# Turning X on VectorE and masking the keys on GpSimd in the levels of a delta-rule scan

## The reference

```python
a_mat = jnp.eye(CHUNK) + jnp.einsum('bhnid,bhnjd->bhnij', kb, kc) * decay * strict   # kb = k * beta
sol = lax.linalg.triangular_solve(a_mat, rhs, left_side=True, lower=True)
attn = jnp.einsum('bhnid,bhnjd->bhnij', qc, kc) * decay

def step(S, xs):                       # per chunk
    v_new = u_c - w_c @ S
    o_c = qd_c @ S + att_c @ v_new
    S = S * gt_c + kt_c.T @ v_new
```

## Time and profile before

| | us |
|---|---|
| median of 3 runs | 1614.75 |
| lowest, highest | 1612.74, 1620.44 |
| the profiled execution | 1610.06 |
| its span | 1608.2 |

### The profile page before, as it was taken

How to read it: one execution, slowest core, us unless ns; L and a number is a source line. 1 busy time by engine, 2 the same in 40 slices (tenths; PEclk the granted TensorE clock), 3 DMA queues, 4 the chain that set the end, 5 groups by cost and what they waited for, 6 DMA issues and landing times.

```text
span 1608.2 us, 33676 instructions
## 1 busy us (share of the span) xinstructions
PE 1552.5 (97%) x13961; PEld 1473.6 (92%) x13961; DVE 1064.3 (66%) x1529; ACT 798.2 (50%) x1200; POOL 372.0 (23%) x387
## 2 busy tenths in 40 slices
PE   6999999899899999999999999999999999999998
PEld 6898989699899999988899999999996799899998
DVE  6785456473888835755888748665557866676653
ACT  7764343554555545454555545444444256653432
POOL 0014443005156620003266421221100000211210
PEclk9999899999999999999999999999999999999999
DMA  7463120354455353642455455555743543455553
GB/s 269 160 190 102 44 69 3 112 182 169 185 181 182 135 180 128 244 143 79 161 181 173 162 200 209 191 176 171 241 157 105 210 150 139 157 175 192 183 168 120
DMA packets 44367, 256.50 MB, mean 159 GB/s; under 512 B 5680, under 2 KB 7840, under 8 KB 21984
## 3 DMA queue, kind: packets, MB, share of 16 engines
q1 hardware_dynamic: 39696, 233.26, 41.9%
q0 software_dynamic: 4416, 20.60, 4.4%
q10 hardware_dynamic: 144, 1.05, 0.2%
HBM read 252.68 MB, written 2.22 MB: 158 GB/s over the span
## 4 chain that ended last, share of the span: by engine, by line
PE 78%; DVE 8%; issue 7%; ACT 4%; DMA 2%; POOL 1%; ACTq 0%; DVEq 0%; SPq 0%; POOLq 0%
PE bank L437 21%; PE bank L438 21%; PE bank L439 21%; PE bank L1264 3%; DVE w_lo L310 2%; ACT w_hi L307 2%; DMA sq<-rows_scratch_q 1%; PE bank L641 1%; DVE rs L594 1%; DVE mix L600 1%; PE bank L1434 1%; DVE w_spare L1337 0%; PE bank L1426 0%; PE bank L1441 0%; PE bank L455 0%
## 5 line engine op out<-in xcount | busy, mean ns | idle before, releaser
L437 PE MATMUL bank<-work_r,w_hi 128*128 128x256 f32 (+2 forms) x3232 | 918.2, 284 | 10.2 <-DVE w_lo L310 6.0
L438 PE MATMUL bank<-work_r,w_hi 128*128 128x256 f32 (+2 forms) x3232 | 909.9, 282 | 0.0
L439 PE MATMUL bank<-work_r,w_lo 128*128 128x256 f32 (+2 forms) x3232 | 909.7, 281 | 0.0
L310 DVE TENSOR_TENSOR w_lo<-ring,w_hi 128x2048 fp32r<-128x2048 f32 (+1 forms) x231 | 497.3, 2154 | 313.4 <-ACT w_hi L307 313.3
L437 PEld LDWEIGHTS bank<-work_r,w_hi 128*128 128x128 f32 x3232 | 610.0, 189 | 23.4 <-issue 12.0
L307 ACT ACTIVATE w_hi<-ring 128x2048 fp32r<-128x2048 f32 (+1 forms) x231 | 408.0, 1767 | 445.3 <-PE bank L439 445.2
L438 PEld LDWEIGHTS bank<-work_r,w_hi 128*128 128x128 f32 x3232 | 609.8, 189 | 0.3
L439 PEld LDWEIGHTS bank<-work_r,w_lo 128*128 128x128 f32 x3232 | 609.6, 189 | 0.0
L1652 POOL TENSOR_TENSOR work<-work 128x272 f32<-128x272 f32 (+1 forms) x44 | 92.6, 2104 | 131.1 <-ACT work L1614 131.1
L1640 DVE SCALAR_TENSOR_TENSOR work<-work,params_sb 128x272 f32<-128x272 f32 (+1 forms) x176 | 99.5, 606 | 5.1 <-DVE work L1640 0.2
L550 POOL TENSOR_TENSOR sq<-sq 128x256 f32<-128x256 f32 (+2 forms) x36 | 53.5, 1487 | 171.9 <-ACT sq L526 170.9
(11 more groups left out here) (450 smaller groups left out, 1685.4 us busy)
## 6 DMA issues: line engine op xcount, KB each, us to landing
ring<-in_stream SPq DMA_DIRECT2D x170, 1024.0 KB, 4.9
ring<-in_stream SPq DMA_DIRECT2D x64, 704.0 KB, 4.0
work<-rows_scratch POOLq DMA_DIRECT2D x12, 512.0 KB, 5.9
ring<-in_stream SPq DMA_DIRECT2D x7, 512.0 KB, 3.9
work<-mem_scratch POOLq DMA_DIRECT2D x3, 1024.0 KB, 5.1
work<-rows_scratch POOLq DMA_DIRECT2D x4, 544.0 KB, 5.9
work<-rows_scratch_o POOLq DMA_DIRECT2D x1, 2176.0 KB, 8.7
ring<-in_stream SPq DMA_DIRECT2D x2, 768.0 KB, 4.2
```

The costliest lines, as they stand in the source:

```text
L310: eng.tensor_tensor(w_lo[:, slot, 0:size], raw_w, w_hi[:, slot, 0:size].bitcast(F32), ALU.subtract).then_inc(lo_done, 1)
L437: pe.matmul(out, w_hi[:, slot, at:at + P], hi, start=first, stop=False)
L438: pe.matmul(out, w_hi[:, slot, at:at + P], lo, start=False, stop=False)
L439: mm = pe.matmul(out, w_lo[:, slot, at:at + P], hi, start=False, stop=last)
```

## The change

In levels 1 to 4, VectorE's transpose instruction turns X in one instruction for each chunk: it turns each 32x32 block in place, which is the whole transpose as long as X is block diagonal with blocks of at most 32. TensorE's `turned` stays for level 5 alone. The mask moves from the product to its operand: GpSimd multiplies A by the level's mask ahead of each level (`level_keys_pool`, 128x256, 10 a group), into two buffers that alternate (`level_a`, `level_b`). With the mask gone from Y, ScalarE copies Y out of PSUM. The masks are no longer turned by TensorE at the start but copied by ScalarE.

```diff
         def first_act(act):
             ahead_exp(act, 0, 1)
-            act.wait_ge(*S.at("first_pe", "masks"))
             ahead_exp(act, 0, 2)
             for s in HALVES:
                 inc(act.activation(level0[s, :], lvl[s, 0, s], ACT.Copy))
+                inc(act.activation(masks[s], lvl[s, 1:TOP, s], ACT.Copy), "masks" if s.start else None)
...
-            inc(act.activation(below, ps[7][:, 0:320].rearrange("p (a b) -> p a b", b=64), ACT.Copy), "masks")
...
+        def level_keys_pool(pool, g, c, l):
...
+            if l > 2:
+                pool.wait_ge(*S.at("scan_pe", f"Y{c}.{l - 2}", g))
+            S.inc(pool.tensor_tensor(level_keys(c, l), A64[c], over(masks[:, l - 1, :], 4), ALU.mult), "level_pool", f"A{c}.{l}")
...
         def ahead_pool(pool, g):
...
             if g > 0:
+                for c in CHUNKS:
+                    level_keys_pool(pool, g - 1, c, 3)
                 pool.wait_ge(*S.at("scan_dve", "attn1", g - 1))
             for c in CHUNKS:
                 inc(pool.tensor_tensor(buf[c]["dec"], bc[:, 8:12, t0:t0 + n], over(cn("causal")[:, 0:P], 4), ALU.add), f"add{c}")
+                if g > 0:
+                    for ck in CHUNKS:
+                        level_keys_pool(pool, g - 1, ck, 3 + c)
...
                 inc(pool.tensor_tensor(XT64[c], over(ident64, 4), XT64[c], ALU.subtract), f"XT{c}")
+                level_keys_pool(pool, g, c, 1)
+            for c in CHUNKS:
+                level_keys_pool(pool, g, c, 2)
...
         def group_dve(dve, g, last):
...
             for l in range(1, TOP):
-                for c in CHUNKS:
-                    dve.wait_ge(*S.at("scan_pe", f"Y{c}.{l}", g))
-                    inc(dve.tensor_tensor(Yc[c], packed(bank(c, 0)), over(below[:, l - 1, :], 4), ALU.mult), f"Y{c}.{l}")
                 beside[l][0]()
                 for c in CHUNKS:
                     dve.wait_ge(*S.at("scan_pe", f"XX{c}.{l}", g))
                     inc(dve.tensor_tensor(X64[c], X64[c], packed(bank(c, 2)), ALU.subtract), f"X{c}.{l}")
+                if l < TOP - 1:
+                    for c in CHUNKS:
+                        dve.wait_ge(*S.at("scan_dve", f"X{c}.{l}", g))
+                        inc(dve.transpose(flat(XT64[c]), flat(X64[c])), f"XT{c}.{l}")
                 beside[l][1]()
...
         def group_act(act, g, last):
...
             for l in range(1, TOP):
                 for c in CHUNKS:
-                    act.wait_ge(*S.at("scan_pe", f"XT{c}.{l}", g))
-                    if l < TOP - 1:
-                        inc(act.activation(XT64[c], packed(bank(c, 1)), ACT.Copy), f"XT{c}.{l}")
...
-                if l in (3, 4) and not last:
-                    ahead_exp(act, g + 1, l - 2)
+                    act.wait_ge(*S.at("scan_pe", f"Y{c}.{l}", g))
+                    inc(act.activation(Yc[c], packed(bank(c, 0)), ACT.Copy), f"Y{c}.{l}")
+                    if l in (3, 4) and not last:
+                        ahead_exp(act, g + 1, l - 2, (0, 1) if c == 1 else (2, 3))
...
         def group_pe(pe, g, last):
...
+                pe.wait_ge(*S.at("level_pool", f"A{c}.{l}", g))
+                inc(by_halves(pe, bank(c, 0), level_keys(c, l), X64[c]), f"Y{c}.{l}")
...
                         pe.wait_ge(*S.at("scan_dve", f"X{c}.{l - 1}", g))
-                        turned(c, l - 1)
                     by_x(c, l)
```

More of the change, by code:

```diff
@@ L674, in program @@
         in_half = area(2048, 7, 64, of=spare)
-        below, level0, ident64 = in_half[:, 0:5, :], in_half[:, 5, :], in_half[:, 6, :]
+        masks, level0, ident64 = in_half[:, 0:5, :], in_half[:, 5, :], in_half[:, 6, :]
         HALVES = (slice(0, 64), slice(64, P))
@@ L688, in program @@
         Yc, XT64 = halves_of("Y")
-        X64, _ = halves_of("X")
+        X64, level_a = halves_of("X")
+        level_b, _ = halves_of("free")
         vb0, ktl0 = area(rows_at + 4, HV, P), area(6144, HV, P, of=spare)
@@ L1113, in first_pe @@
             first_xx_pe(pe, L0 - 1)
[L1114 to L1117, removed]
             of_qkv(30).was_read(pe)
@@ L1180, in fetch_rows, with level_keys @@
             pool.dma_start(dst, src).then_inc(S.sem(f"{kind}_in"), 16)
+        def level_keys(c, l):
+            return (level_a if l % 2 else level_b)[c]
+        def level_keys_pool(pool, g, c, l):
+            if (c, l) == (1, 1):
+                S.begin("level_pool")
+            if l > 2:
+                pool.wait_ge(*S.at("scan_pe", f"Y{c}.{l - 2}", g))
+            S.inc(pool.tensor_tensor(level_keys(c, l), A64[c], over(masks[:, l - 1, :], 4), ALU.mult), "level_pool", f"A{c}.{l}")
         def ahead_pool(pool, g):
@@ L1221, in ahead_pool @@
                 inc(pool.tensor_tensor(XT64[c], over(ident64, 4), XT64[c], ALU.subtract), f"XT{c}")
+                if g == 0 and c == 1:
+                    pool.wait_ge(*S.at("first_act", "masks"))
+                level_keys_pool(pool, g, c, 1)
+            for c in CHUNKS:
+                level_keys_pool(pool, g, c, 2)
             arrived("eG")
@@ L1236, in ahead_keys_dve, with ahead_exp @@
                           f"A{c}" if cols != rows else None)
-        def ahead_exp(act, g, c):
-            if c == 1:
+        flat = lambda v: v.rearrange("p h n -> p (h n)")
+        def ahead_exp(act, g, c, heads=range(4)):
+            if c == 1 and 0 in heads:
                 S.begin("ahead_act")
             act.wait_ge(*S.at("ahead_pool", f"add{c}", g))
-            for h in range(4):
+            for h in heads:
                 v = buf[c]["dec"][:, h, :]
                 ins = act.activation(v, v, ACT.Exp, bias=colv[:, c, 1, 4 * g + h:4 * g + h + 1])
-            S.inc(ins, "ahead_act", f"dec{c}")
+            if 3 in heads:
+                S.inc(ins, "ahead_act", f"dec{c}")
         def ahead_x_act(act, g, c):
@@ L1368, in group_act @@
                 for c in CHUNKS:
-                    act.wait_ge(*S.at("scan_pe", f"XT{c}.{l}", g))
-                    if l < TOP - 1:
-                        inc(act.activation(XT64[c], packed(bank(c, 1)), ACT.Copy), f"XT{c}.{l}")
[L1372 to L1376, removed]
-                if l in (3, 4) and not last:
-                    ahead_exp(act, g + 1, l - 2)
+                    act.wait_ge(*S.at("scan_pe", f"Y{c}.{l}", g))
+                    inc(act.activation(Yc[c], packed(bank(c, 0)), ACT.Copy), f"Y{c}.{l}")
+                    if l in (3, 4) and not last:
+                        ahead_exp(act, g + 1, l - 2, (0, 1) if c == 1 else (2, 3))
+            for c in CHUNKS:
+                act.wait_ge(*S.at("scan_pe", f"XT{c}.{TOP - 1}", g))
+                if g == 0 and c == 1:
+                    act.wait_ge(*S.at("first_zeros"))
+                for s in HALVES:
+                    inc(act.activation(buf[c]["XT"][s, :, s], packed(bank(c, 1))[s], ACT.Copy), f"XT{c}.{TOP - 1}" if s.start else None)
             def new_values(c):
@@ L1412, in product @@
             def product(c, l):
[L1413 removed]
+                pe.wait_ge(*S.at("scan_act", f"Y{c}.{l}", g))
                 if l > 1:
[L1415 removed]
+                    pe.wait_ge(*S.at("scan_dve", f"XT{c}.{l - 1}", g))
                 elif g > 0:
@@ L1501, in scan_pool @@
                     first_zeros_pool(pool)
+            for l in range(3, TOP):
+                for c in CHUNKS:
+                    level_keys_pool(pool, GROUPS - 1, c, l)
         def scan_dve(dve):
```

3 lines of the change are left out of this document (1 added, 2 removed).

## The result

| | us |
|---|---|
| changed kernel, median of 20 runs | 1622.66 (1615.65 to 1627.84) |
| kernel before, 20 runs beside them | 1616.97 (1610.37 to 1622.82) |
| ratio of the runs | 1.0042, 95% interval 1.0029 to 1.0055 |
| span of the profiled execution | 1620.5 (before 1608.2) |

The change costs 5.7 us by the two medians and 6.8 by the ratio. The forecast was 1610.1.

A forecast was written before the change was run, and what follows sets the result against it. TensorE, busy 97% of the span, was taken as the bound. Gains of 0.95, 0.4, 0.4 and 2.9 us in groups 0 to 3 sum to -4.65, from 1614.75 to 1610.1 us; range 1603.5 to 1618.5.

The forecast's parts named there:

- A level, 2.32 us: One undisturbed scan level, the chain of one chunk from Y to subtraction with hand-overs: falls from 3.07 to 2.32 us.
- The transposes, 0.42: VectorE's new transposes in the levels: 0.42 us each, starts 0.33 apart, hidden with some 0.6 us to spare.
- The rival of slow transposes: VectorE's transposes come 0.6 us apart, so attn1 is 0.5 later: gain only 1.9 us, 1612.9; chance 0.12.
- the rival in which they wait for GpSimd as well: VectorE's transposes wait for GpSimd's products: up to 1 us a level, up to 10 us for the scan, 1625; chance 0.08.
- Group 0, 0.95 us less: Scan of group 0, TensorE at 1.2 GHz until 174: a `turned` falls out ahead of Y, attn1 comes earlier, gain 0.95.
- Group 3, 2.9 us less: Last group, no next group's work: Y of level 2 to keys-times-state from 12.01 to 9.03 us, less 0.06 at level 1.
- the late copy of Y: Level 1: ScalarE, busy with the values, copies Y late; Y of level 2 at 205.80 instead of 205.74, gain 0.
- The stall of level 3, 2.4 us, gain 0.4 us in groups 1 and 2: Y's copy of chunk 2 queues behind exponentials awaiting GpSimd's add; TensorE holds 2.4 us, leaving 0.4 us gain a group.
- the sentence on the decayed state: VectorE's decayed state before the last subtractions: may take 1.5 us as before, ending before `turned` of level 5 starts.
- The clock: Rival: TensorE's clock falls in the level 3 stall, from pauses of some 2.3 us: some 2.8 us a group; chance 0.24.
- "No stall", -12.5 us, chance 0.08: Rival: waits on GpSimd's add cost little; 2.9 us gained a group, 3.8 in group 0: -12.5, 1602.3; chance 0.08.

The follow-up runs named there:

- keys_exp: Changed kernel, ScalarE's exponentials behind both copies of levels 4 and 5, GpSimd's level 4 keys ahead of its wait for attn1: 28.86 us a group, ratio 0.9944.
- filler_decay: Changed kernel with four unused batches on TensorE in the pause of level 3, and the decayed state on ScalarE: 31.52 and 31.53 us in groups 0-1, 1-2.
- decay_act: Changed kernel with the decayed state made by ScalarE behind its level 5 copies, not VectorE: 32.32 and 32.22 us in groups 0-1, 1-2; ratio 0.9996.
- filler2: Changed kernel with four unused batches on TensorE between keys-times-state and the turn of level 5, groups 0 and 1: 34.39 us in groups 0-1, 1-2.
- keys4_only: Changed kernel with only GpSimd's order altered, level 4 keys ahead of its wait for attn1: 33.35 and 33.57 us in groups 0-1, 1-2.
- exp_behind: Changed kernel with ScalarE's exponentials behind both copies of levels 3 and 4, as before the change: 38.33 and 37.94 us in groups 0-1, 1-2.
- best: keys_exp plus ScalarE's values of chunk 2 moved behind its copies of level 1: 27.99 us a group, ratio 0.9912, median 1602.22 us.

## Why the prediction was wrong

The time from one keys-times-state to the next, groups 0 and 1, in us, can be laid out as steps from run to run. Each term is the difference of two runs, so that they add up by their making:

| | us |
|---|---|
| both queues in a good order (keys_exp) | 28.86 |
| the stall of level 3 and the small waits of level 4, at full clock (filler_decay less keys_exp) | +2.66 |
| the clock's fall behind it (decay_act less filler_decay) | +0.75 |
| VectorE's wait for GpSimd (filler2 less decay_act) | +2.1 |
| the clock's fall behind that (changed less filler2) | +2.6 |
| changed | 37.0 |

- **A level, 2.32 us:** it is 2.37. Right.
- **The transposes, 0.42:** they are 0.44 and 0.40. Right. The estimate of 0.44 from the Trainium skill ("VectorE: DVE Perf Modes", The three transpose paths) agrees with the trace too. Its own figure of 311 ns for two-byte elements is shown by no run here, and the 0.13 us that was added for 128 more columns is half of the step from the subtraction's 0.42 to `attn`'s 0.69; by the subtraction's own rate (0.33 for 256) it would be 0.17. The rival of slow transposes falls, and the rival in which they wait for GpSimd as well, with 14 of the 32 beside one of its products. By the rule that the prediction cites from the Trainium skill ("SBUF — State Buffer", Who interferes with whom), the instruction with two SBUF inputs was the one at risk, and the trace agrees: it took up to 4.10 us, the transposes at most 0.44.
- **Group 0, 0.95 us less:** from its first Y to keys-times-state it took 16.73 us and takes 16.04, 0.7 less, with a fall of the clock in it.
- **Group 3, 2.9 us less:** 2.53. Three levels take 0.05 more each, level 5 (Y to keys-times-state) 2.25 in place of 2.07, and level 1 loses 0.12 in place of 0.06. The pause of 0.9 us at level 1 was in the forecast, as the late copy of Y.
- **The stall of level 3, 2.4 us, gain 0.4 us in groups 1 and 2:** the pause is 2.21 us, in all of groups 0 to 2. With that stall, but without VectorE's wait and without a fall of the clock, a group takes 31.5 us (filler_decay), 0.2 under the 31.7 of before. The mechanism was right (keys4_only leaves the stall at 2.21), and so was that the gain is eaten there; the size was near.
- **The step that failed is the sentence on the decayed state:** "it may take 1.5 us as before, which ends at about 218.1, and `turned` of level 5 starts at 218.8 anyway". The 1.5 us was taken as the duration of one meeting with one GpSimd instruction. In groups 0 and 1 it is the time to the next gap in GpSimd's run, and the change closes the gap: the exponentials of both chunks are now done before GpSimd needs them, so kn, decb, decb and qn run without a break. It took 4.1 and 4.0 us in these two groups: 2.1 us each on the path, and 2.6 more by the clock behind it. 9.4 us in all, where the sum had nothing. The prediction held both sides of the meeting: its own decayed state starts at about 216.6 and its own kn, decb and qn end at about 221.3. It priced GpSimd's port for the transposes, as a rival, and not for the one instruction that its rows already showed at 1.49 against 0.685 us.
- **The clock** was named as the way to the slower side, with a chance of 0.24 and 2.8 us a group. It fell with the stall in all three groups, but there it cost 0.75 us: it was low for 3.4 us, and few batches stand on the chain before it is back. The dear fall, 2.6 us, came behind the pause that I had not seen. Both pauses (2.2 and 2.0 us) are shorter than the 2.3 us from which the prediction let it fall, read from one earlier pause: what it had read there was the moment of the fall, and not the shortest pause that has one. Here TensorE had begun again when the fall came, in all but the first of group 0. Pauses of 1.53 us (exp_behind) and 1.09 (keys4_only) had none behind them, as the 1.6 of the earlier trace rows.
- **"No stall", -12.5 us, chance 0.08:** another order of two queues comes near it: keys_exp measured -9 us, best -13. Part of keys_exp's gain is that its decayed state happened to fall in a gap.

What stays open is group 2. In the changed kernel the decayed state got through there in 0.84 us, between two decb that ran back to back:

```profile
257.70 0.84 DVE L1342 TENSOR_TENSOR work<-w_spare 128x512 f32<-128x512 f32 x1
256.72 2.95 POOL L1222 TENSOR_TENSOR w_spare<-w_spare,work 128x512 f32<-128x512 f32 x2
```

The two decb take 2.49 us elsewhere, 0.46 less, and the decayed state ends some 0.56 us after the time at which the first would be done. It is the same in group 2 of all eight kernels that have the transposes and leave this product on VectorE (0.84 to 1.68 us): it waits for the one GpSimd instruction beside it and gets in before the next, which ends 0.46 late. In groups 0 and 1 it met the run in six of these kernels, and in all twelve cases it waited to the end of the run. One difference is that GpSimd fetches rows before and behind its run in groups 0 and 1 and fetches none in group 2; whether that decides was not tried.

## What to carry to other kernels

An instruction of VectorE with two SBUF inputs may have no duration of its own beside a busy GpSimd: here it took from one GpSimd instruction (group 2) to a whole run of four (groups 0 and 1), and such a run should be priced at its full length. Whoever gives GpSimd more work, or makes what it waits for earlier, closes gaps, and should look for every such instruction on VectorE. ScalarE with a scale took the same product, placed later, and no copy of it was longer than 402 ns. And work of the next group that waits for a third engine belongs behind, not between, the two copies for which TensorE waits. With GpSimd's keys of level 4 moved ahead of its wait, that turned a loss of 0.4% into a gain of 0.6% (keys_exp). Either queue alone did not: 38.1 us a group with the exponentials moved behind the copies of levels 3 and 4 (exp_behind), 33.5 with the keys alone.

## What the runs showed of the hardware that was not expected

- The decayed state (128x512, two SBUF inputs) took 0.65 us in a gap and up to 5.76 us beside four GpSimd instructions without a gap between them, even where it began 0.28 us ahead of the first. In groups 0 and 1 it never got in between two that ran back to back; in group 2 it always did, at 0.84 to 1.68 us.
- Filling one pause of TensorE kept the clock up and won nothing, as the end of the next wait was set by GpSimd's run; filling the other won 2.6 us a group (one run) with work that nobody reads.
- The two falls of the clock cost 0.75 and 2.6 us. In the first it was low for 3.4 us over small batches that wait on each other, in the second for 6.8 us over dense products; how much of the difference is the time and how much the work was not measured apart.
